# A ring of half-size slots and released-in-order down weights in a two-layer network on one core

## What is computed

```python
h = layer_norm(concatenate([meta, x]), ln_emb_g, ln_emb_b)      # 528 x 1024
for l in range(2):
    parts = split(h @ w_in[l])       # q, k, v, gate of a retention; a pooling input; q, k, v, forget gates
    mix = concatenate([retention(...), pooling(...), forgetting_attention(...)])
    h = layer_norm(ALPHA * h + mix @ w_out[l], ln1_g, ln1_b)
    y = (silu(h @ w1[l]) * (h @ w3[l])) @ w2[l]                  # 1024 -> 2816 -> 1024
    h = layer_norm(ALPHA * h + y, ln2_g, ln2_b)
return h[16:]
```

## Time and profile before

| | |
|---|---|
| median of 3 runs | 3274.61 us (3264.3 to 3277.98) |
| profiled execution | 3272.24 us |
| its span in the trace | 3270.1 us |
| first block and embedding | 0 to 1740 us |
| the two layers | 1740 to 3270 us |
| busy share of the span: PE, DVE, ACT, POOL | 94%, 36%, 17%, 1% |
| mean granted clock of TensorE | 0.965 |
| DMA | 743.71 MB, 227 GB/s over the span |

### The profile page before, as it was taken

The page is one execution under the profiler, slowest core; times in us unless marked ns, Lnnn a source line. Parts: engine busy times, 40 slices in busy tenths (PEclk is TensorE's granted clock), DMA queues, the critical chain, the costliest instruction groups (busy, mean ns, idle before and its releaser), DMA issues.

```text
span 3270.1 us, 52738 instructions
## 1 busy us (share of the span) xinstructions
PE 3080.4 (94%) x22521; PEld 1730.5 (53%) x22521; DVE 1163.1 (36%) x2350; ACT 545.3 (17%) x1133; POOL 47.4 (1%) x58
## 2 busy tenths in 40 slices
PE   9878989799999999999989999998999989999999
PEld 3355545233333334333445668573786648675766
DVE  1633355222222222232363452527044342435131
ACT  1332320111111111111122221130112100130000
POOL 0000002000000000000010000000000000000000
PEclk9878989899999999999989999999999999999999
DMA  9800125899999999999853333324333243343442
GB/s 400 351 1 30 49 84 220 319 409 407 410 402 408 407 406 406 405 409 408 356 234 125 118 132 113 144 109 162 148 121 147 103 193 129 116 162 116 180 158 100
DMA packets 97467, 743.71 MB, mean 227 GB/s; under 512 B 11128, under 2 KB 38336, under 8 KB 57552
## 3 DMA queue, kind: packets, MB, share of 16 engines
q1 hardware_dynamic: 58768, 687.49, 53.1%
q10 hardware_dynamic: 32624, 30.52, 2.9%
q0 software_dynamic: 5968, 24.14, 1.9%
HBM read 674.98 MB, written 67.13 MB: 227 GB/s over the span
## 4 chain that ended last, share of the span: by engine, by line
PE 55%; DMA 26%; DVE 4%; ACT 2%; issue 1%; ACTq 1%; POOL 1%; DVEq 0%
DMA arena<-x_sorted 24%; PE psum L1648 19%; PE psum L1632 10%; PE psum L1577 5%; PE psum L1281 3%; PE psum L1588 3%; PE psum L1356 2%; PE psum L839 1%; PE psum L1392 1%; ACTq L597 1%; PE psum L1233 1%; PE psum L857 1%; PE psum L1679 1%; PE psum L1448 1%; DMA x_sorted<-arena 1%
## 5 line engine op out<-in xcount | busy, mean ns | idle before, releaser
L1281 PE MATMUL psum<-weight_ring,arena 128*32 128x512 f32 x6192 | 677.5, 595 | 42.8 <-DVE arena L2936 42.1
L1648 PE MATMUL psum<-arena,weight_ring 128*128 128x256 f32 (+1 forms) x2816 | 636.8, 385 | 5.7 <-ACT arena L2291 5.7
L1648 PEld LDWEIGHTS psum<-arena,weight_ring 128*128 128x128 f32 x2816 | 529.4, 190 | 102.2 <-issue 11.9
L1281 PEld LDWEIGHTS psum<-weight_ring,arena 128*32 128x32 f32 x6192 | 199.9, 110 | 500.7 <-issue 458.4
L1356 PE MATMUL psum<-weight_ring,arena 128*32 128x256 f32 x6144 | 338.2, 380 | 0.0
L1356 PEld LDWEIGHTS psum<-weight_ring,arena 128*32 128x32 f32 x6144 | 196.6, 110 | 153.0 <-issue 26.8
L2958 DVE STREAM_TRANSPOSE arena<-arena 128x384 f32<-128x384 f32 x32 | 18.6, 580 | 632.8 <-DMA arena<-x_sorted 632.8
L1632 PE MATMUL psum<-weight_ring 128*128 128x512 f32 x468 | 206.7, 600 | 10.1 <-DMA weight_ring<-weights 8.0
L3273 DVE TENSOR_TENSOR weight_ring<-weight_ring,psum 128x256 f32<-128x256 f32 (+1 forms) x88 | 37.4, 425 | 423.2 <-PE psum L1648 420.5
L1577 PE MATMUL psum<-weight_ring,arena 128*128 128x512 f32 (+2 forms) x512 | 175.0, 500 | 3.1 <-ACT arena L2291 3.1
L1632 PEld LDWEIGHTS psum<-weight_ring 128*128 128x128 f32 x468 | 89.5, 192 | 123.7 <-issue 118.6
(11 more groups left out here) (446 smaller groups left out, 2678.5 us busy)
## 6 DMA issues: line engine op xcount, KB each, us to landing
weight_ring<-exp_gu SPq DMA_DIRECT2D x129, 2048.0 KB, 11.6
weight_ring<-weights SPq DMA_DIRECT2D x104, 2048.0 KB, 7.9
weight_ring<-exp_down SPq DMA_DIRECT2D x64, 2048.0 KB, 11.1
x_sorted<-arena SPq DMA_DIRECT2D x2, 10752.0 KB
arena<-x_sorted ACTq DMA_DIRECT2D x132, 96.0 KB, 22.2
y_sorted<-arena ACTq DMA_DIRECT2D x128, 96.0 KB, 17.4
y_sorted<-arena SPq DMA_DIRECT2D x2, 5632.0 KB, 39.4
y_sorted<-arena SPq DMA_DIRECT2D x2, 5120.0 KB, 37.8
```

Source lines behind the costliest of these rows:

```text
L1281: mm = pe.matmul(psum[j * GROUP:(j + 1) * GROUP, g, :], xg[:, k // 4, g, k % 4 * GROUP:(k % 4 + 1) * GROUP], w[:, kk, j * 512:(j + 1) * 51 ...
L1648: mm = pe.matmul(bank[:, 0:b - a], w[:, k, col:col + P], h2_t[:, k, a:b], start=(k == 0), stop=(k == KT - 1))
```

## The change

The weight ring is kept in eight half-size slots of 1 MB. A `Stream` object hands out pieces of one or two slots, and SP waits, for each piece, for every earlier piece whose slots it takes. The w2 weights are laid out in column halves: a down half has six pieces of 1 MB, the three of column half 1 first, then the three of column half 0. Column half 1 is freed after product p3 (and DVE's fourth right sums), column half 0 and, in a mix, the first w_out piece after p5. PE waits for single pieces where it first uses them. The wait for the last up product moves to the last pair of p2. `DOUBLE_STEPS` gets shorter and `DOWN_STEPS` goes. DVE's mid norms become a generator, `mid_norms`: after the mix of (0, A) one row tile follows each feature read of `project`; elsewhere all follow the mix as before. At the end of a down half 1 all tiles are centred before the first is scaled. ACT takes the root of tile 2 after both tiles of (1, B) are turned. The diff, cut to its core:

```diff
-DOUBLE_STEPS = dict(A=(4, 5, 6, 7, 8, 12), B=(5, 6, 7))
-DOWN_STEPS = (0, 2)
+DOUBLE_STEPS = dict(A=(4, 5, 6), B=())
...
+class Stream:
+    def __init__(self, ring, landed):
+        self.ring, self.landed, self.arrived = ring, landed, [0] * HALF_SLOTS
+        self.pieces, self.at = [], 0
+    def ask(self, source, size):
+        slot = self.at % HALF_SLOTS
+        assert slot + size <= HALF_SLOTS
+        self.arrived[slot] += 16
+        piece = Piece(source, self.at, size, self.ring[:, slot * HALF:(slot + size) * HALF], (self.landed[slot], self.arrived[slot]))
+        self.pieces.append(piece)
+        self.at += size
+        return piece
+    def before(self, piece):
+        places = {p % HALF_SLOTS for p in range(piece.at, piece.at + piece.size)}
+        found = []
+        for earlier in reversed(self.pieces[:self.pieces.index(piece)]):
+            own = {p % HALF_SLOTS for p in range(earlier.at, earlier.at + earlier.size)}
+            if own & places:
+                found.insert(0, earlier)
+                places -= own
+        return found
...
             def weights(l, n):
-                at = len(stream)
-                stream.append(l * LAYER_PIECES + n)
-                pe.wait_ge(layer_landed[at % LAYER_SLOTS], 16 * (at // LAYER_SLOTS + 1))
-                return slot[at % LAYER_SLOTS], at
+                return stream.ask(("weights2", l * LAYER_PIECES + n), 2)
+            def down_weights(l, c, half, n):
+                return stream.ask(("down2", ((l * 2 + c) * DOWN_PIECES // 2 + n) * 2 + half), 1)
...
-                products(("mixed", l, x), KT // 2, pair_view(h2_t, 0, KT // 2, x), mix_blocks(ws), ready={"p2": fox_outs})
-                for at in ats:
-                    piece_free[at] = main.done()
-            def products(key, pairs, left, right, ready={}, steps=None, pace=()):
+                products(("mixed", l, x), KT // 2, pair_view(h2_t, 0, KT // 2, x), mix_blocks(ws), [ws[0]] * 2, [ws[1]], fox_outs.rest)
+            def products(key, pairs, left, right, first, second, left_whole):
...
-                        if q == pairs - 1 and name in ready:
-                            ready[name].rest(pe)
+                        if n == 0 and name == "p1":
+                            first[part].wait(pe)
+                        if q == pairs - 1 and name == "p2":
+                            left_whole(pe)
...
+                    if name == "p3":
+                        for piece in second:
+                            piece.free = [main.done(), (right_ready, parts + 4 * len(right))]
+                for piece in first:
+                    piece.free = [main.done()]
...
             def feed_down(l, x, c, steps):
                 a, b = span(l, x)
                 f0, f1 = FF_CHUNKS[c]
-                pe.wait_ge(*main.drained_of(("up", l, x, f1 - 1)))
-                ws = [weights(l, W_DOWN + 3 * c + n) for n in range(3)]
-                views = [w.rearrange("p k n -> p (k n)").rearrange("p (k n) -> p k n", k=4) for w, _ in ws]
                 if in_products(l, x, c):
-                    mark["down", l, x, c] = [at for _, at in ws]
+                    second, first = ([down_weights(l, c, half, n) for n in range(DOWN_PIECES // 2)] for half in (1, 0))
+                    halves = mark["down", l, x, c] = [first, second]
...
+                            if f % 4 == 0:
+                                for half in range(2):
+                                    halves[half][f // 4].wait(pe)
+                            if f == f1 - f0 - 1:
+                                last_ready(pe)
...
+                    pe.wait_ge(*main.drained_of(("up", l, x, f1 - 2)))
                     pairs = (f1 - f0) // 2
-                    products(("down", l, x, c), pairs, pair_view(ff_t, 0, pairs, x, a), down_blocks([w for w, _ in ws], c),
-                             steps=steps, pace=DOWN_STEPS if c else ())
-                    for _, at in ws:
-                        piece_free[at] = main.done()
+                    products(("down", l, x, c), pairs, pair_view(ff_t, 0, pairs, x, a), down_blocks(halves, c), first, second, last_ready)
                     return
...
+                pe.wait_ge(*main.drained_of(("up", l, x, f1 - 1)))
+                halves = [[down_weights(l, c, half, n) for n in range(DOWN_PIECES // 2)] for half in range(2)]
                 for half, t in rows_items(l, x):
                     each(steps)
                     bank = main.bank(pe)
                     for f in range(f1 - f0):
-                        w = views[f // 4][:, f % 4, :]
+                        piece = halves[half][f // 4]
+                        if f % 4 == 0:
+                            piece.wait(pe)
...
+                    for piece in halves[half]:
+                        piece.free = [main.done()]
...
-            for n, piece_id in enumerate(stream):
-                if n == 0:
-                    sp.wait_ge(sem("early_slots_free"), 1)
-                elif n == LAYER_SLOTS - 1:
+            sp.wait_ge(sem("early_slots_free"), 1)
+            for piece in stream.pieces:
+                if piece.at == 2 * (LAYER_SLOTS - 1):
                     sp.wait_ge(*mark["embedded"])
-                elif n >= LAYER_SLOTS:
-                    sp.wait_ge(*piece_free[n - LAYER_SLOTS])
-                at = n % LAYER_SLOTS
-                sp.dma_start(ring[:, at * PIECE:(at + 1) * PIECE], io["weights2"][piece_id]).then_inc(layer_landed[at], 16)
+                for earlier in stream.before(piece):
+                    for free in earlier.free:
+                        sp.wait_ge(*free)
+                name, index = piece.source
+                sp.dma_start(piece.flat, io[name][index]).then_inc(piece.landed[0], 16)
...
-                turn_rows("mid", 1, "B", (last,))
+                turn_rows("mid", 1, "B", (None, last))
...
+                        each(norms)
...
+            def mid_norms(l, x):
                 for t in rows_of(l, x):
                     norm_rows(V, h2[0:SIZE[t], t, :], t, ln_par2, sem("mid_ready"), SIZE[t], first_half=(t == 0))
+                    yield
...
-                    if c == 1:
-                        each(steps, len(DOWN_STEPS))
-                    for at in ats:
-                        landed_piece(dve, at)
+                    for piece in halves[1] + halves[0]:
+                        piece.wait(dve)
...
-                        for t in rows_of(l, x):
-                            norm_scaled(norm_centered(t), sem("layer_start"), parts)
+                        for both in [norm_centered(t) for t in rows_of(l, x)]:
+                            norm_scaled(both, sem("layer_start"), parts)
...
-                project(0, "B", items=(SPLIT_B, 99))
+                project(0, "B", items=(SPLIT_B, 99), norms=mid_norms(0, "A"))
...
                 mix(0, "B", 3)
+                each(mid_norms(0, "B"), NT2)
...
+        w2 = w2.reshape(DOWN_PIECES, 4, P, 2, 512).transpose(0, 3, 2, 1, 4)
+        down.append(w2.reshape(DOWN_PIECES * 2, P, HALF))
+    io = {"weights2": np.concatenate(pieces), "down2": np.concatenate(down)}
```

More of the change, by code:

```diff
@@ L1597, in mix @@
                 pe.wait_ge(*fox_outs.drained_of(("fox", l, x, 3)))
-                ws, ats = zip(*(weights(l, W_OUT + half) for half in range(2)))
-                mark["mix", l, x] = ats
+                ws = [weights(l, W_OUT + half) for half in range(2)]
+                mark["mix", l, x] = ws
                 if 0 in rows_of(l, x):
```

88 lines of the change are left out of this document (48 added, 40 removed).

## The result

The changed kernel takes **3248.43 us**, the median of 5 runs (3239.48 to 3248.88), against 3274.61 us before (3264.03 to 3277.98, 5 runs). The ratio is 0.9924, with a 95% interval of 0.9900 to 0.9948. The forecast was 3254.5 us, range 3238 to 3268.

A forecast was written before the change was run, and what follows sets the result against it. TensorE, busy 94% of the span, was taken as the bound, with at most 60 us idle to win in the layers. Terms -1.1 + 3.5 + 4.2 + 3.1 + 1.3 + 5.0 + 4.1 = 20.1 us gave 3254.5 us, range 3238 to 3268.

The forecast's parts named there:

- 1a: Layer 0, rows A, down then mix of rows B: weight wait goes, PE waits for DVE's norms instead; 1.1 us lost.
- 1b: The same place after layer 0, rows B, with two norm rows: idle 4.8 us instead of 8.1; gain 3.5 us.
- 1c: Layer 1, rows A, second down half: halves land at T + 5.3 and T + 8.0, T ending the preceding products; gain 4.2 us.
- 2: Later down-half starts: six waits of 0.51 to 0.53 us for the last up product go; gain 3.1 us.
- 3: After the mix of layer 0, rows A: norms interleaved with feature reads; gain 2.9 less 1.6, so 1.3 us.
- 4: Feed stages: one attention step per feature chunk removes four waits for attention weights; gain 5.0 us, cost taken as nothing.
- 5: Turn of layer 1, rows B: ScalarE's root of row 2 after both turned rows shortens PE's 3.65 us idle; gain 4.1 us.
- Rival A: Only the weights were late: the three waits return 32 us and the rest 13.5; 3229 us; 6%.
- B: Attention chain comes into the open: each of 24 units waits up to 1.7 us; 3300 us; 4%.
- C: Clock keeps what the waits give: stops get shorter but not fewer; sum 14 us, 3261 us; 20%.
- D: 1 MB lands no sooner than 2 MB: second half at T + 16; sum 12 us, 3262 us; 5%.
- E: Slots don't come free early, but DVE is awaited anyway in the two mixes, so no cost; 3255 us, within the forecast.

The follow-up runs named there:

- e1: Changed kernel, but column half 1 is freed with the rest after p5 instead of after p3; layers 1510.7 us against 1501.8 in the changed kernel.
- e2: Changed kernel with the late release after p5 and PE awaiting all pieces at each block's head, 1 MB halves kept; layers 1521.0 us against 1501.8.
- e5: Changed kernel with the old attention steps (two steps in some feature chunks); layers 1508.8 us against 1501.8 in the changed kernel.
- e7: Changed kernel with the three middle norms of layer 0, A, done together ahead of the feature reads, as before; layers 1500.4 us against 1501.8.
- after: The profiled execution of the changed kernel itself, no further edit; 3239.48 us, layers 1501.8 us against 1528.7 before the change.
- e3: Changed kernel with column half 1 of the output weights asked for ahead of half 0; layers 1501.0 us against 1501.8 in the changed kernel.
- e9: Changed kernel with the wait for the last up product back at the start of each down half; layers 1505.1 us against 1501.8.

## Why the prediction was right, and where it was not

The sum was 20.1 us and the layers gave 26.9; the medians differ by 26.2. Step by step:

- **1a** (-1.1): place 1 went from 65.2 to 65.7 us, -0.5 (65.2 to 66.7 in the other executions with the same wait). p7 started at T + 16.2 (16.0 predicted) after 9.16 us idle (9). The clock cost was 2.1, not 2.7 us. Right, and e1 and e2 show that the ring has no part in it.
- **1b** (+3.5): 65.3 to 62.4 us here, +2.9, and 60.9 in other executions, +4.4. Taken together with the stretch behind it, where the clock puts the difference, and less part 2's 0.6, it is 4.7. Idle 4.94 us (4.8). Right in mechanism, somewhat under-sized.
- **1c** (+4.2): 65.4 to 59.4, **+6.0, under-sized**. The first half landed at T + 5.05 (5.3 predicted) and the wait was 3.17 us (3.5). But the second wait of 1.3 us did not come: the instructions behind the stop ran at a granted clock of 0.77 and then 0.50, so that they lasted beyond the second landing, T + 7.6 by e5. The clock cost was 1.9 us (2.2 predicted): 26 instructions took 13.18 us, where 30 take 13.04 at full rate. The Trainium skill, "DMA: Bandwidth & Descriptors", section "Anatomy of one DMA — SWDGE (gpsimd) path", gives T + 6.8 for the second landing by the prediction's estimate, which counts its fixed part once, and T + 8.8 if it is counted for each half. The measured 7.6 lies between them and near the 8.0 from the rows. (The rows' landings lie 4.9 to 5.0 us apart once the 0.4 us between the issues are counted, not 4.7; for the halves this changes 0.2 us.) From T + 11 on the granted clock was 1.00 again. The Trainium skill, "TensorE: Matmul & The Clock Gate", section "HAM oscillation — how this bites in real kernels", describes bursts between DMA waits as staying slow; this one did not.
- **2** (+3.1): about 3.7, since the skipped waits cost 0.6 and not 0.5 each. The cover it lends to the heavy step (1.6 us late predicted, 1.7 measured) was right, but the step is late once, at (0, B), c = 0, and not twice.
- **3** (+1.3): the stretch gave 3.6 us with 0.6 of part 2, so 3.0 here, but none in the executions at the longer length. The step it names, 1.5 us at the second transpose, measured 1.76, and at the same clock e7 gives 1.3. That this is the forecast's number is luck: the forecast was 2.9 less 1.6 for slow matmuls, while after and e7 have none there.
- **4** (+5.0): 5.5, the waits and little clock. Right in size; but **its cost was not nothing by itself**. The prediction moved the step's DVE and PE work and did not follow ACT's loads of bias rows in it. They land later now (10.3 us, before 5.7); the early release keeps that off PE.
- **5** (+4.1): 4.2, though the mechanism was half another: 1.8 of it is DVE's new order, which I had costed at nothing everywhere. That the number fits is partly luck, since the stage could have come out 1.7 us shorter by its clock.
- Some 1.5 us more lie in the projection of (1, B), whose code is the same: its first 50 us have a granted clock of 1.00 in after, 0.97 before and 0.97 in e1 and e3. This is the other side of 1b.

**Rival A** (the weights are the only thing late) is out: the waits for DVE are there at their predicted lengths. **B** is out, no wait for attention weights is left. **C** (3261 us) had a grain: the clock took 2.1, 3.1 and 1.9 us at the three places, about as much as the sum allowed for (2.7, 2.5 and 2.2). **D** is out by the landings at T + 5.1 and T + 7.6. **E** was part of the forecast and is **wrong**: late release costs nothing at 1a and 1b, as it said, but 8.9 us in the layers, 6.4 of them in waits for attention weights that stand behind the bias rows. The total didn't show this, since the change has the early release.

So most of the release order's worth isn't where its weights are waited for. At the three places it gives nothing that e1 can show; it spreads the loads, so that the bias rows land in time for the new steps.

## What to carry to other kernels

When a wait for data ends, look up what the consumer's other inputs do in that time: here VectorE's norms stood ready only just before, and removing the weight wait of 8 us gave -0.5 us until the norms were moved too (then 11 us). When a step is moved, follow its small loads as well as its arithmetic: behind a burst of large ones they landed three times later here. And an engine that serves two chains in a fixed order, as ScalarE with its roots, passes the wait of one chain to the other; look at its order after each improvement.

## What the runs showed of the hardware that I had not expected

- The price of a stop did not follow its length. The stop of 9.15 us at place 1 and that of 4.94 us at place 2 occur in eight executions each (after, e1, e3, e5 to e9), and each was followed by a loss of 1.6 to 3.1 us in the next 40 instructions, sometimes the longer stop by more, sometimes the shorter. Behind the stops of 8.0 and 8.1 us before the mixes of the old kernel it was 2.7 us. So a shortened stop gave back its length and little clock.
- The same instructions with the same waits took one of two lengths, 1.5 to 3.0 us apart, at three places. The granted clock of these stretches differs (0.85 or 0.92, 0.98 or 1.00, 0.97 or 1.00), and at place 2 what one stage loses the next one has back. Why it falls at one time and not at another is open.
- 264 KB loads took 5.7 us (median) where they were asked for ahead of a burst and 18.2 us where they were asked for behind three 2 MB loads of another engine's queue.
